# The first norm of a two-layer decoder reads a turned copy of x instead of turning x on TensorE

## What is computed

```
for i in range(DEPTH):                      # 2
    h = _rmsnorm(x, norm[i])
    x = x + (_fox_attention(h, ...) if i == 0 else _dilated_attention(h, ...))
    x = x + square(relu(_rmsnorm(x, mlp_norm[i]) @ mlp_w1[i])) @ mlp_w2[i]
```

## Time and profile before

| | |
|---|---|
| median of 3 runs | 1524.58 us (1524.36 to 1524.78) |
| the profiled execution: its own time | 1524.63 us |
| its span in the trace | 1522.6 us |
| TensorE busy in it | 1512.8 us |
| first product of the projection starts | 8.69 us |
| VectorE, ScalarE, GpSimd busy | 934.8, 701.5, 376.4 us |

### The profile page before, as it was taken

The page is one execution under the profiler, slowest core; times in us unless marked ns, Lnnn a source line. Parts: engine busy times, 40 slices in busy tenths (PEclk is TensorE's granted clock), DMA queues, the critical chain, the costliest instruction groups (busy, mean ns, idle before and its releaser), DMA issues.

```text
span 1522.6 us, 24820 instructions
## 1 busy us (share of the span) xinstructions
PE 1512.8 (99%) x9304; PEld 1230.6 (81%) x9312; DVE 934.8 (61%) x1659; ACT 701.5 (46%) x1191; POOL 376.4 (25%) x499
## 2 busy tenths in 40 slices
PE   9999999999999999999999999999999999999998
PEld 7777777888888888888878877887878888888887
DVE  5467644556474769745646486655556475655678
ACT  6434354453544536545444343534453553535353
POOL 3301100220110511353327154324622210101010
PEclk9999999999999999999999999999999999999999
DMA  6221201477565754432223422232315466566753
GB/s 183 74 80 43 71 29 51 145 145 199 118 181 132 172 148 94 152 101 80 70 84 85 127 56 84 70 83 71 104 66 192 113 138 193 110 193 124 198 120 84
DMA packets 111600, 173.57 MB, mean 114 GB/s; under 512 B 12688, under 2 KB 45456, under 8 KB 111504
## 3 DMA queue, kind: packets, MB, share of 16 engines
q1 hardware_dynamic: 91904, 134.51, 28.7%
q0 software_dynamic: 17408, 33.56, 13.7%
q10 hardware_dynamic: 2192, 4.20, 0.8%
HBM read 165.89 MB, written 6.36 MB: 113 GB/s over the span
## 4 chain that ended last, share of the span: by engine, by line
PE 97%; DVE 1%; ACT 1%; DMA 0%; POOL 0%; issue 0%; SPq 0%; ACTq 0%; POOLq 0%
PE ps L657 63%; PE ps L979 20%; PE ps L791 3%; PE ps L736 3%; PE ps L764 3%; PE ps L803 2%; PE ps L704 1%; PE ps L781 1%; PE ps L728 1%; DMA w_raw<-in_fox_w_in 0%; PE ps L748 0%; ACT p_sb L1136 0%; PE ps L687 0%; PE ps L732 0%; DVE w_l L1391 0%
## 5 line engine op out<-in xcount | busy, mean ns | idle before, releaser
L657 PE MATMUL ps<-w_h,act_h 128*128 128x512 f32 x768 | 308.3, 401 | 1.8 <-DVE w_l L1866 1.1
L657 PE MATMUL ps<-w_h,act_l 128*128 128x512 f32 x768 | 301.7, 393 | 0.0
L657 PE MATMUL ps<-w_l,act_h 128*128 128x512 f32 x768 | 301.4, 392 | 0.0
L1395 DVE SCALAR_TENSOR_TENSOR w_l<-w_raw,gain_t,w_h 128x512 fp32r<-128x512 f32 x186 | 140.7, 798 | 100.8 <-ACT w_h L1059 100.7
L657 PE MATMUL ps<-act_h,w_h 128*128 128x512 f32 x512 | 199.6, 390 | 0.0
L657 PE MATMUL ps<-act_l,w_h 128*128 128x512 f32 x512 | 199.2, 389 | 0.0
L657 PE MATMUL ps<-act_h,w_l 128*128 128x512 f32 x512 | 199.2, 389 | 0.0
L1927 POOL TENSOR_TENSOR qrs<-qss,m_half 128x8 f32<-128x8 f32 x64 | 111.3, 1739 | 312.0 <-DVE qss L1447 311.7
L657 PEld LDWEIGHTS ps<-w_h,act_h 128*128 128x128 f32 x768 | 152.2, 198 | 30.6 <-issue 3.4
L657 PEld LDWEIGHTS ps<-w_l,act_h 128*128 128x128 f32 x768 | 152.1, 198 | 28.0
L979 PE MATMUL ps<-w_h,op_h 128*128 128x512 f32 x448 | 174.4, 389 | 0.0
(11 more groups left out here) (229 smaller groups left out, 2409.7 us busy)
## 6 DMA issues: line engine op xcount, KB each, us to landing
w_raw<-in_dil_w_in SPq DMA_DIRECT2D x72, 512.0 KB, 3.7
raw<-in_mlp_w SPq DMA_DIRECT2D x64, 512.0 KB, 4.8
raw<-in_mlp_w POOLq DMA_DIRECT2D x48, 512.0 KB, 5.8
w_raw<-in_mlp_w SPq DMA_DIRECT2D x32, 512.0 KB, 5.1
w_raw<-in_fox_w_in SPq DMA_DIRECT2D x22, 512.0 KB, 3.7
p_sb<-in_mlp_w SPq DMA_DIRECT2D x16, 512.0 KB, 5.2
pT_sb<-in_mlp_w SPq DMA_DIRECT2D x16, 512.0 KB, 5.8
w_raw<-in_mlp_w POOLq DMA_DIRECT2D x16, 512.0 KB, 7.2
```

What stands on the lines that cost most here:

```text
L657: return mm(ps_out, lhs[i], rhs[j], start=(k == 0 and term == 0), stop=(k == KT - 1 and term == 2))
L1395: last = v.scalar_tensor_tensor(w_l[u % WR][:, j, :], raw(u)[:, j, :], gain_t[:, norm, k:k + 1], f(w_h[u % WR][:, j, :]), ALU.mult, ALU.su ...
```

## The change

The host lays out a second copy of x, `x_t`, in which each token tile has channels in partitions. Its four tiles (512 KB each) are loaded into `qT[1]` and `kT[1]`, which nothing else uses until the second set of heads. ScalarE and VectorE make `act_h` and `act_l` of the first norm from there, and TensorE's 32 transposes of x are gone. x itself is still loaded, for the sums of squares and the residual, but behind the first weights. The sums of tiles 2 and 3 move from ahead of the step into ScalarE's event for bank 1, ahead of that bank's split and behind tile 3's copy.

```diff
-            for what, n in (("x", 0), ("w", 0), ("w", 1), ("w", 2), ("w", 3), ("x", 1), ("x", 2), ("x", 3)):
+            sp.dma_start(x_turned(0)[:, 0:D // 2], x_t[0, :, 0:D // 2]).then_inc(xt_first, 16)
+            for what, n in (("w", 0), ("x_t", 0), ("w", 1), ("w", 2), ("w", 3), ("x_t", 1), ("x", 0), ("x", 1), ("x_t", 2), ("x", 2), ("x_t", 3), ("x", 3)):
...
-                            if k == (6 if b == 0 else 3) and b + 1 < NT:
-                                prepare(0, 0, b + 1)
-                                prepare(0, 1, b + 1)
...
-            keep_busy(6)
-            prepare(0, 0, 0)
-            prepare(0, 1, 0)
-            keep_busy(8)
+            keep_busy(20)
...
-                act.wait_ge(prep_full, prep_no(n, t, half) + 1)
+                if n == 0:
+                    act.wait_ge(xt_first if t == 0 and half == 0 else xt_in[t], 16)
+                    nc.scalar.copy(prep_dst(n, half, t)[0], x_turned(t)[:, half * 512:half * 512 + 512]
+                                   .rearrange("p (k t) -> p k t", k=4)).then_inc(acth_done, 1)
+                    return
+                act.wait_ge(prep_full, prep_full_no(n, t, half))
...
                         if s == 0 and b < 2:
                             prepare(0, 0, b + 2)
                             prepare(0, 1, b + 2)
+                        if s == 0 and b == 1:
+                            norm_sum(0, 2)
+                            norm_sum(0, 3)
                         bank_event(s, b, attend)
...
-            for t in range(NT):
-                norm_sum(0, t)
-                if t == 0:
-                    prepare(0, 0, 1)
-                    prepare(0, 1, 1)
+            prepare(0, 0, 1)
+            prepare(0, 1, 1)
+            norm_sum(0, 0)
+            norm_sum(0, 1)
             step(*STEPS_FOX[0])
...
+    laid["x_t"] = laid["x"][0].reshape(NT, P, KT, P).transpose(0, 3, 2, 1).reshape(NT, P, D)
```

## The result

The changed kernel takes 1534.74 us (median of 6 runs, 1534.24 to 1535.24) where the kernel before took 1524.49 on the same chip (6 runs, 1524.33 to 1524.81). The ratio is 1.0067 [1.0057, 1.0077]: slower by 10.25 us. The profiled execution took 1534.24 us, 9.6 more than that of before. The forecast was 1533.5, range 1530.3 to 1535.3, slower.

The account below looks back on a forecast made before the run. TensorE was taken to bound the kernel, with 97% of the chain that ended last. A 7.4 us wait for unit 4 plus 1.5 for slow pace gave 8.9 on 1524.63: 1533.5 us, own range 1531.8 to 1534.3, stated 1530.3 to 1535.3.

Parts of the forecast that it names:

- The transposes: TensorE: three groups between products leave at 0.79 us each, 2.37 in all; 2.15 us gained by the turn.
- the turn: TensorE turning bank 0's queries (L803), at 27.62 before; forecast at 34.95, after waiting for VectorE's `qn`.
- the first group: First eight transposes between products, ahead of bank 1: forecast to bring 0.57 of its 0.79 us.
- The start: Turned tile 0's second half delays the first product to 9.6, 0.9 us late; bank 1 starts near 15.7.
- The queue: SyncE's loads: four more transfers, 2.10 MB at 408 GB/s, delay unit 4 by 5.1 us, to 25.1.
- The rival in which the DMA engines would serve it in time: Unit 4 lands at 20.0 beside the new loads, turn at 29.85, 1526.8 to 1528.3 us; chance 0.07.
- What waits for unit 4: ScalarE's split, square, tile 3 copy and two sums, then GpSimd and VectorE: turn at 34.95, costing 7.3 us.
- The room of 1.8 us: Bank 0's `qn` was ready at 25.83, 1.8 us before TensorE turned it in the kernel before.
- The next turn: Bank 1's queries: `qn` ready at 40.1, TensorE there at 40.2; no second wait, narrowly, 0 to 0.3 us.
- The pace: TensorE after its pause of over 9 us: slow clock for 2.9 us costs 1.5 us, ends 0 and 2.
- The rival in which the clock stays: No slow pace after TensorE's pause: 7.4 us slower, 1532.0 (1530.3 to 1532.3); chance 0.17.
- the case of more than one wait: Next turn also waits, or units 6 and 7 come late for bank 4: 1535.5 to 1537.5 us; chance 0.08.

Follow-up runs that it names:

- The queue alone: Kernel before, with the four tiles of x loaded a second time (512 KB each, unread) right behind the last tile of x: 1530.06 us, ratio 1.0037.
- the wait filled: Changed kernel with unused identity products on TensorE ahead of the turn of bank 0's queries, 38 or 46: 1532.77 us and 1532.91 us.
- 38 products: Changed kernel with 38 more identity products on TensorE right ahead of the turn of bank 0's queries, results unused: 1532.77 us, ratio 1.0057.
- both faults undone: Changed kernel with the sums of tiles 2 and 3 ahead of unit 4's split and units 4 and 5 ahead of the small loads: 1526.49 us, ratio 1.0011.
- the sums back: Changed kernel with the sums of squares of tiles 2 and 3 ahead of unit 4's split on ScalarE again: 1530.44 us, ratio 1.004.
- the units early: Changed kernel with units 4 and 5 issued right behind the last tile of x, ahead of the small loads: 1530.71 us, ratio 1.004.

## Why the prediction was right, and which term was mis-sized

**The transposes.** They left TensorE and gave nearly what was forecast: TensorE was at the turn at 25.70 (forecast 25.5), 1.9 us early instead of 2.15. The parts were further off than their sum. Bank 1 started at 16.18 (forecast 15.7), so the first group brought 0.09 us and not 0.57; from there to the turn TensorE needed 9.5 us where the forecast had 9.8, so the other two brought 1.8 and not 1.58.

**The start.** First product at 10.03, forecast 9.6. Two terms were short: the copy of half a tile ended at 7.97, not 7.5, since it began at 7.35 rather than 6.96 and took 0.62 rather than 0.53. The forecast had let the half tile arrive when the same number of bytes had been through before; it came 0.4 later. Bank 1 was late by much the same, 0.5. This cost nothing in the end, as TensorE then waited 10 us for something else.

**The queue: right in kind, mis-sized.** This is the step that was off, "I take 5.1, since SyncE's queue issued units 4 and 5 only after the large loads had gone through". ScalarE's split came at 26.18, forecast 25.1, so the shift was 6.1 us against 20.11. Where the missing microsecond lies is seen in DMA traffic, microsecond by microsecond (last column GB/s), first of the kernel before, then of the changed one:

```profile
13.00:14.00 1.00, 1.00 (x6) 0.75 (x5) 0.74 (x2) 0.33 (x2) 0.00 (x0) 1.00 1.10 328
14.00:15.00 1.00, 1.00 (x10) 0.99 (x9) 0.00 (x0) 0.35 (x1) 0.00 (x0) 1.00 1.19 63
...
18.00:19.00 1.00, 1.00 (x10) 0.87 (x9) 0.00 (x0) 0.91 (x2) 0.00 (x0) 1.00 0.91 324
```

```profile
19.00:20.00 1.00, 1.00 (x6) 0.84 (x5) 0.00 (x0) 0.00 (x0) 0.00 (x0) 1.00 1.26 161
...
24.00:25.00 1.00, 1.00 (x6) 0.82 (x5) 0.00 (x0) 0.00 (x0) 0.00 (x0) 1.00 0.96 313
```

At some 400 GB/s the large loads end near 13.95 before and near 19.4 after: 5.4 us, of which 5.1 were forecast. The stretch in which only small loads run, until the next row above 300, begins 5.4 us later and ends 6 us later; so the small loads have grown by 0.6, where the forecast held that they could only shrink (its lower end, 4.5). SyncE's queue shows the same. Units 4 and 5 were issued at 22.04, where the forecast had 20.5. The last gain ahead of them was issued at 20.34, 5.55 after 14.79 before, and its issue took 1.66 us where it had taken 0.58; why it is longer behind more loads is open. The queue alone, measured in the kernel before, moved the split by 5.6.

**Unit 4 behind, not beside, the new loads.** The rival in which the DMA engines would serve it in time would have put the split at 20.0; it was 6.2 later. The Trainium skill, DMA: Bandwidth & Descriptors, section Queues, rings and completion order, says that a DMA engine takes one queue's descriptors in ring order; all of these loads are in SyncE's queue, and the splits at 26.18 here and 25.71 with the queue alone agree with it.

**What waits for unit 4.** From the split to the turn the forecast had 9.85 us (25.1 to 34.95) and the trace has 9.86. Each link was worked out from rows of before, and their sum held: of the turn's 1.09 us over its forecast, 1.08 are unit 4's landing. The room of 1.8 us was read rightly too: the queue alone moved the split by 5.6 and the turn by 3.87.

**The next turn.** No second wait, as forecast, but not as narrowly: `qn` of bank 1 was ready at 41.13 (forecast 40.1) and TensorE came at 42.72, not 40.2, since the slow pace, which that paragraph left out, made it later.

**The pace.** Forecast 1.5 us, from the program's head; measured 1.44 between the turns, 1.3 to 1.8 with the wait filled. The rival in which the clock stays is out. The evidence was indirect, since at the head the granted clock reads 1.00 while the pace is half; after the wait it shows. Stretches of the changed kernel:

```profile
25.70:36.00 10.30, 0.16 (x1) 0.00 (x0) 2.94 (x6) 6.87 (x12) 2.76 (x4) 0.65 0.25 52
36.00:39.10 3.10, 3.06 (x10) 2.60 (x11) 3.06 (x7) 1.85 (x4) 0.77 (x1) 0.51 0.42 152
39.10:42.70 3.60, 3.60 (x17) 2.93 (x16) 2.69 (x6) 0.90 (x2) 1.73 (x2) 1.00 0.48 145
```

The clock falls during the rest and is at 0.51, the 1.2 GHz level, for the first 3.1 us of work. The Trainium skill, TensorE: Matmul & The Clock Gate, Part 1, calls the throttled clock the state at rest; these rows agree.

**The sum.** Forecast 7.4 + 1.5 = 8.9; measured 8.42 + 1.44 = 9.9 in the span and 9.6 in the profiled execution's time, as 1.7 us lie outside the span now and 2.0 did before. The forecast was 0.7 us short of that execution and 1.2 of the median. Nearly all of that is the queue's term: the wait, 8.42, lies above its stated end of 7.7, and the median lies above the forecast's own range, which ended at 1534.3. It lies within the stated 1535.3 only because the range had been widened for the case of more than one wait, which did not happen. That part is luck; the mechanism is not.

## What to carry over

Before a load is put into an in-order queue that is already full, look at what stands behind it there and at who waits for that; four loads of 512 KB nobody waited for cost this kernel 5.6 us. Work that is moved off an engine's early list lands behind whatever that list waits for later, and the two costs nearly add. And what the bound engine gets back is worth only the room of the chain that feeds its next step: here the 1.9 us by which TensorE got ahead could not come out before SyncE's list, ScalarE's and the place of the turn were changed, and then 2.0 came out by the medians and 1.1 in the trace.

## What the hardware showed beyond what was expected

**A short rest can bring the slow clock.** Rests of 1.98 us (with 38 products) and 2.62 us (with both faults undone) were followed by the 1.2 GHz level in the traced executions and, by the times, not in others of the same kernels, which were 1.7 and 1.9 us quicker and have no trace. In those traces the turn and the products just behind it ran at full pace, and the clock fell 1.1 to 1.3 us after work had resumed. The length doesn't decide it alone: the changed kernel's rest of 2.13 us ahead of its first product at 10.03 was followed by products at 10.33 and 10.56, the full pace.

**In these traces a longer rest wasn't dearer in pace.** The second turn comes 5.24 us behind the first at full pace. After a rest of 10.18 us it came after 6.68 (1.44 more), but after 3.81, 6.20 and 7.23 us it came after 7.72, 7.51 and 7.70: 2.3 to 2.5 more. In the kernel with the sums back, work resumed at 31.96 and the clock still read 0.50 at 35 to 36 us. These are single executions. Those behind the three dearer figures took 0.7, 0.5 and 1.4 us more than the medians of their kernels, that behind the 1.44 took 0.5 less, and executions of one kernel lay up to 2.3 us apart, so the price of a rest is not settled by them. What decides how long the clock stays low was not tried.

**An issue gets longer with the loads ahead of it.** SyncE's issue of the one load at L632 (`b_f`, L618 before) took 3.49 us before, 6.44 with four more large loads ahead of it, and 6.25 with the same loads added to the kernel before. A queue's rows show traffic, then, and not only the work of issuing. Unit 4, issued at 10.2 to 10.5 in all kernels with the units early, was waited for until 23.0 to 23.2 in five of the six traces and split at 21.60 (0.20 us idle) in that with both faults undone. Why it landed 1.4 us earlier there stays open.
